# Expert blocks of 1792 columns in place of 896 in the MoE stage of a two-layer decoder trunk

## The reference

```
def swiglu(x, w_gate, w_up, w_down):
    return (jax.nn.silu(x @ w_gate) * (x @ w_up)) @ w_down

def moe_swiglu(x, w_router, w_gate, w_up, w_down):
    top_vals, top_idx = lax.top_k(logits, TOP_K)
    ...
    for e in range(N_EXPERTS):
        out = out + gates[..., e:e + 1] * swiglu(x, w_gate[e], w_up[e], w_down[e])
```

## Time and profile before

| | us |
|---|---|
| median of 3 runs | 1392.83 |
| lowest and highest run | 1390.17, 1393.66 |
| the profiled execution's own time | 1392.43 |
| its span in the trace | 1390.7 |
| first product of the expert stage to the last down matmul | 451.79 to 1352.9 |
| PE, DVE, ACT busy, share of the span | 96%, 83%, 71% |

### The profile page before, as it was taken

One profiled execution on the slowest core, in us unless ns is written; L12 is line 12 of the kernel. 1 busy time (PEld: TensorE's weight loads), 2 busy tenths in 40 slices (PEclk: granted clock), 3 DMA queues, 4 the chain that ended last, 5 costly groups with the idle time before them and its releaser, 6 DMA issues.

```text
span 1390.7 us, 19504 instructions
## 1 busy us (share of the span) xinstructions
PE 1332.4 (96%) x6863; PEld 1145.8 (82%) x6863; DVE 1147.9 (83%) x1052; ACT 990.2 (71%) x959; POOL 96.9 (7%) x112
## 2 busy tenths in 40 slices
PE   9999999999999999999999999999999998999987
PEld 8988888888997887878779888788888887787865
DVE  5776554466665898999999999999999999899986
ACT  5555444446555777888978888888888898787884
POOL 2000000000000086300000000000000002000000
PEclk9999999999999999999999999999999999999999
DMA  9657855567542799999999999999999999999980
GB/s 321 238 164 277 287 195 182 182 218 229 181 137 72 284 355 415 409 411 412 391 409 396 411 411 412 400 412 410 410 412 409 402 412 409 411 409 397 397 351 30
DMA packets 137062, 454.51 MB, mean 327 GB/s; under 512 B 8233, under 2 KB 29749, under 8 KB 124718
## 3 DMA queue, kind: packets, MB, share of 16 engines
q1 hardware_dynamic: 130272, 429.95, 80.6%
q0 software_dynamic: 4832, 17.13, 3.4%
q10 hardware_dynamic: 1902, 6.70, 1.4%
HBM read 437.99 MB, written 15.75 MB: 326 GB/s over the span
## 4 chain that ended last, share of the span: by engine, by line
PE 56%; DMA 18%; DVE 13%; issue 7%; ACT 5%; SPq 1%; ACTq 0%; DVEq 0%
PE banks L1228 15%; PE banks L1777 13%; DVE w_lo L2000 10%; DMA raw<-in_o_exp_down 8%; DMA raw<-in_o_exp_gate 7%; PE banks L1262 6%; PE banks L1798 5%; PE banks L1536 4%; PE banks L1850 4%; PE banks L1814 3%; ACT w_hi L684 3%; DMA raw<-in_e_w_in 1%; DMA raw<-in_o_exp_up 1%; PE banks L1761 1%; SPq L394 1%
## 5 line engine op out<-in xcount | busy, mean ns | idle before, releaser
L2000 DVE TENSOR_TENSOR w_lo<-raw,w_hi 128x1792 fp32r<-128x1792 f32 (+1 forms) x454 | 919.6, 2063 | 123.4 <-PE banks L1228 50.0
L684 ACT ACTIVATE w_hi<-raw 128x1792 fp32r<-128x1792 f32 (+1 forms) x454 | 784.1, 1736 | 273.3 <-PE banks L1228 79.7
L1798 PE MATMUL banks<-w_lo,x_hi 128*128 128x448 f32 x512 | 131.5, 379 | 18.7 <-DVE w_lo L2000 18.4
L1798 PEld LDWEIGHTS banks<-w_lo,x_hi 128*128 128x128 f32 x512 | 91.0, 188 | 45.4 <-DVE w_lo L2000 39.5
L1777 PE MATMUL banks<-w_hi,x_hi 128*128 128x448 f32 x512 | 127.5, 371 | 0.0
L1777 PE MATMUL banks<-w_lo,x_hi 128*128 128x448 f32 x512 | 125.1, 366 | 1.8 <-DVE w_lo L2000 1.8
L1798 PE MATMUL banks<-w_hi,x_hi 128*128 128x448 f32 x512 | 125.4, 367 | 0.0
L1777 PE MATMUL banks<-w_hi,x_lo 128*128 128x448 f32 x512 | 124.7, 365 | 0.0
L1228 PE MATMUL banks<-w_hi,x_lo 128*128 128x512 f32 (+1 forms) x304 | 108.5, 357 | 0.3 <-DVE x_lo L2035 0.3
L1228 PE MATMUL banks<-w_hi,x_hi 128*128 128x512 f32 (+1 forms) x304 | 108.1, 356 | 0.0
L1228 PE MATMUL banks<-w_lo,x_hi 128*128 128x512 f32 (+1 forms) x304 | 108.1, 356 | 0.0
(11 more groups left out here) (340 smaller groups left out, 1827.3 us busy)
## 6 DMA issues: line engine op xcount, KB each, us to landing
raw<-in_o_exp_gate SPq DMA_DIRECT2D x128, 896.0 KB, 8.1
raw<-in_o_exp_up SPq DMA_DIRECT2D x128, 896.0 KB, 8.8
raw<-in_o_exp_down SPq DMA_DIRECT2D x96, 1024.0 KB, 8.4
raw<-in_o_exp_down SPq DMA_DIRECT2D x32, 512.0 KB, 7.9
raw<-in_o_w_qkv SPq DMA_DIRECT2D x12, 1024.0 KB, 5.2
raw<-in_e_ffn_gate SPq DMA_DIRECT2D x11, 1024.0 KB, 5.1
raw<-in_e_ffn_up SPq DMA_DIRECT2D x11, 1024.0 KB, 5.3
raw<-in_e_ffn_down SPq DMA_DIRECT2D x11, 1024.0 KB, 5.0
```

The source lines that it names most:

```text
L684: act.activation(w_hi[:, at % HI, 0:size], raw[:, at % RAW, 0:size], ACT.Copy).then_inc(hi_made, 1)
L1798: mm = pe.matmul(bank[first + f][:, 0:CUT // 2], x_two[:, 2 * k + kk, :], w[:, kk, f * (CUT // 2):(f + 1) * (CUT // 2)], start=start and k ...
L2000: ve.tensor_tensor(w_lo[:, at % LO, 0:size], raw[:, at % RAW, 0:size], w_hi[:, at % HI, 0:size], ALU.subtract)\
```

## The change

`CUT` is 1792 and `BLOCKS` 2, so a superstep has 48 tiles and each duo two of them. A gate or up tile is now one 128-row chunk by 1792 columns: the same 896 KB, in rows of 7168 bytes. Tiles, bytes and matmuls of the stage stay as many as they were. A product fills four PSUM banks, gate and up one after the other in the same four; the other four hold the down sums. The loop over blocks is gone: the duo loop holds both supersteps. On ACT and DVE the merged element-wise operations cover twice the columns, in halves where a chain needs them so. The wide sums are cleared by two DVE memsets, where two zero matmuls did it.

The tiles of a superstep stand thus: 0 to 7 wide gate; 8, 9 small down (of the block before); 10 to 17 wide up; 18 to 21 small down; 22 to 29 small gate; 30, 31 small down; 32, 33 wide down; 34 to 41 small up; 42 to 47 wide down. Tiles 19, 31, 33 and 43 are single chunks (512 KB). `turn_wide` stands between 19 and 20, the first `turn_sums` after 31, the second after 43. At a duo's boundary all of `turn_rows` comes before tile 46 in one piece, and so do the ACT and DVE splits of the gathered rows.

```diff
-STEP_TILES = 24
-SKIP = 4
+STEP_TILES = 48
+SKIP = 8
...
-                load(tile_at(i, j, b), w[e, of, :, 2 * k:2 * k + 2], slot=(MOE_T - SKIP + i) % RAW)
+                load(tile_at(i, j, c), w[e, of, :, k:k + 1], slot=(MOE_T - SKIP + i) % RAW)
...
-                for k in range(4):
-                    up(eg, wide, of, k, k, j, b)
-                up(eu, wide, of, 0, 4, j, b)
-                down(small_was, of_was, 0, 5, j, b)
-                up(eu, wide, of, 1, 6, j, b)
-                down(small_was, of_was, 1, 7, j, b)
-                up(eu, wide, of, 2, 8, j, b)
-                up(eu, wide, of, 3, 9, j, b)
...
+                for k in range(KC):
+                    up(eg, wide, of, k, k, j, c)
+                small_down(0, 2)
+                for k in range(KC):
+                    up(eu, wide, of, k, 10 + k, j, c)
+                small_down(2, 6)
+                for k in range(KC):
+                    up(eg, small, of, k, 22 + k, j, c)
+                small_down(6, 8)
+                second_half(wide, small, of, j, c)
...
             with sp.Fori(0, last) as j:
                 wide, small = wide_of(j), small_of(j)
-                blocks(wide, small, j)
+                superstep(wide, 1, small, 0, small, j, 0)
                 sp.wait_ge(jobs_ready, 1)
                 wide, next_small = wide_of(j + 1), small_of(j + 1)
-                superstep(wide, 0, small, BLOCKS - 1, next_small, j, BLOCKS)
+                superstep(wide, 0, small, 1, next_small, j, 1)
...
+            def up_products(base, k, i, j, c, passes, free=None):
...
+                wait_high(tile_at(i, j, c))
+                for n, (x, low) in enumerate(passes):
+                    if low:
+                        wait_tile(tile_at(i, j, c))
+                    for f in range(4):
...
+                        mm = pe.matmul(bank[base + f][:, 0:CUT // 4], x, w[low][:, FOURTHS[f]],
+                                       start=k == 0 and n == 0, stop=k == KC - 1 and n == len(passes) - 1, skip_group_check=True)
+                mm.then_inc(tile_used, 1)
```

More of the change, by code:

```diff
@@ L487, in small_of @@
                 return sp.value_load(job_int[0:1, bass.ds(j + MOST, 1)], min_val=0, max_val=EXPERTS - 1)
[L489 to L497, removed]
+            for k in range(KC):
+                up(eg, 0, 0, k, 8 + k, None, None)
+            for k in range(KC):
+                up(eu, 0, 0, k, 16 + k, None, None)
             sp.wait_ge(ids_ready, 1)
             first_small = sp.value_load(job_int[0:1, MOST:MOST + 1], min_val=0, max_val=EXPERTS - 1)
-            for k in range(4):
-                up(eg, first_small, 0, k, 12 + k, None, None)
+            for k in range(KC):
+                up(eg, first_small, 0, k, 24 + k, None, None)
             second_half(0, first_small, 0, None, None)
@@ new lines, in st, with sts, silu_wide @@
+            def st(i, j, c, final=False):
+                used(i, j, c)
+                split_at(i + HI, j, c, final)
+            def sts(first, last, j, c, final=False):
+                for i in range(first, last):
+                    st(i, j, c, final)
+            def silu_wide(j, c):
+                if j is not None:
+                    act.wait_ge(hidT_ready, step_no(j, c) - 1)
+                for m in range(2):
+                    act.activation(halves(hid)[m], columns(0, m), ACT.Silu).then_inc(e_silu_made, 1)
@@ new lines, in turned_wide, with copy_sums, high_gate @@
+            def turned_wide(j, c):
+                act.wait_ge(hidT_ready, step_no(j, c))
+                for m, (first, last) in enumerate(CHUNKS):
+                    act.activation(hidT_hi[:, first:last], turned(1 if j is None else 0, m), ACT.Copy).then_inc(hidT_hi_made, 1)
+            def copy_sums():
+                for m in range(2):
+                    act.activation(halves_of_sums[m], columns(0, m), ACT.Copy).then_inc(s_copied, 1)
+            def high_gate(j, c):
+                act.wait_ge(fold_ready, 2 * step_no(j, c) - 1)
@@ L1166, in block @@
+                if c:
                     for half in range(2):
@@ L1816, in product @@
                     return mm
[L1818 to L1826 removed]
+                wait_high(tile_at(i, j, c))
+                if t == 7:
+                    wait_tile(tile_at(i, j, c))
@@ new lines, in los, with hidden_wide @@
+            def los(first, last, j=None, c=None, final=False):
+                for i in range(first, last):
+                    lo(i, j, c, final)
+            def hidden_wide(j, c):
+                n = step_no(j, c)
+                ve.wait_ge(tile_used, tile_at(23 if j is None else 17, j, c) + 1)
+                for m in range(2):
+                    ve.wait_ge(e_silu_made, 2 * n - (1 - m))
+                    ve.tensor_tensor(halves(hid)[m], halves(hid)[m], columns(1 if j is None else 0, m), ALU.mult).then_inc(e_hid_made, 1)
@@ new lines, in clear_wide, with second_half @@
+            def clear_wide(j=None):
+                for half in range(2):
+                    if j is not None:
+                        ve.wait_ge(y_made, 2 * j + (half + 1))
+                    ve.memset(bank[6 + half], 0.0).then_inc(wide_cleared, 1)
+            def second_half(j, c, final=False):
+                add_gate(j, c)
+                lo(32, j, c, final)
+                lo(33, j, c, final)
+                if c:
+                    fold_y(j)
+                for n, i in enumerate((34, 36, 38, 40)):
+                    if final:
+                        add_rows(*divmod(n, 2))
+                    los(i, i + 2, j, c, final)
+                lo(42, j, c, final)
+                lo(43, j, c, final)
+                add_up(j, c)
+                hidden_small(j, c)
+                lo(44, j, c, final)
+                low_small(j, c)
+                lo(45, j, c, final)
+                if j is not None and not c and not final:
+                    gathered(0, j + 1)
+                    gathered(1, j + 1)
+                    gathered_small(j + 1)
+                lo(46, j, c, final)
+                lo(47, j, c, final)
```

762 lines of the change are left out of this document (327 added, 435 removed).

## The result

The changed kernel takes **1426.46 us** (median of 4 runs, 1424.38 to 1428.18), the kernel before 1391.91 in the same comparison: 1.024 times as long, 95% interval 1.0218 to 1.0262. I had said 1395, 1376 to 1409. The direction I leaned to was right, the size was not, and the time lies outside my range.

A forecast was written before the change was run, and what follows sets the result against it. Fetch bounds the kernel before; PE and DVE would hide its saving. 100.7 + 753.2 + 19 + 4.8 + 18 = 895.7, plus 5.2 and 1.5, gave 902.4 against 901; +2.5 taken: about 1395 us, range 1376 to 1409.

The forecast's parts named there:

- What bounds before: Steady block of the kernel before: the fetch bounds it, 53.6 us, with PE and DVE 1.5 to 2 us behind.
- Part 1, the fetch: Gate and up rows of 7168 bytes for 3584: 18.4 us less fetch (0 to 25.6) over 16 blocks.
- Part 2: Engines in a long phase: a superstep walks to 107.6 us, so PE and DVE hide the fetch's saving.
- tiles 32 to 47: 36.6: Superstep's end: wide downs 19.2, small up 13 to 15.5 half hidden by the downs, two turns 3; together 36.6 us.
- Part 3: the boundary: Once a duo: fold and memsets 2.2 us, turning 1.4, wait for gathered rows 2.75; together 6.35.
- lump of 1.5 us: Whole stage: added for one more case than now of the granted clock falling behind an idle PE.
- Part 4: opening and tail: Stage's two ends: opening and its second half 100.7 us, tail 18.
- Rival A: Fetch stays the bound, rings carry DVE's lead through small phases: 1374 us, 1367 to 1385; chance 0.27.
- Rival B: Stalls at tiles 22 and 0 with the clock falling behind them, 1.6 us a superstep more: 1408 us; chance 0.18.
- Rival C: Pieces are cut into packets as before, fetch keeps its time: 1393 to 1403 us; chance 0.07.
- The signs I named: In the trace: `silu_wide` starts 107 to 109 us apart, DMA share 0.96 to 0.99, mean packet 5.4 KB or more, among others.
- stalls at every superstep, +1.7: Upper bound of the unknown sizes: 1.7 us more a superstep, +12 in all.

The follow-up runs named there:

- light turning: Changed kernel with 3 splits of gathered rows on ACT and on DVE at the boundary, and 3 transposes for 16 in each superstep: 1410.81 us.
- all light parts: Changed kernel with boundary splits and turning cut, fold at the superstep's end, small gate w_lo on half columns: 1404.58 us; with half of gate and up columns fetched, 1375.43.

## Why the prediction was wrong, step by step

- **What bounds before: right.** The fetch. Halving it gave 37 us; relief of DVE gave nothing. The floor that I read from busy times, 1.5 to 2 us under the fetch in a block, so 6 to 8 a duo, was near the 8.6 measured. But I read the earlier trace rows as evidence: SP's waits on DVE are 227 us before, 237 changed, and 228 with half the fetch. They are the ring's pace, whoever bounds, and tell nothing.
- **Part 1, the fetch: right in kind, 14 for 18.4.** And nearly all of it is hidden in the changed kernel, as said (2.6 us left).
- **Part 2: two thirds of the walk held.** Tiles 0 to 17: 42.6 walked, 19.4 + 3.6 + 19.5 = 42.5 measured. Tiles 18 to 31: 28.3 walked, 28.5 to 29.0 measured, with the wait at tile 22 at 2.0 for 1.7 and DVE's pace through the small gate at 1.9 a tile; moving the low half showed that the wait is DVE's amount of work. **The step that failed is "tiles 32 to 47: 36.6".** With the fold's 2.2 and the turning's 1.4 of part 3, I had 76.8 for them in the two supersteps of a duo; without the boundary's wait they took 82.0 to 83.0, 17 us more over three duos. I summed the work there and named no wait. In the duo from 673.83 there are these: for `add_gate` and the tiles' w_lo 1.2, for `add_up` ahead of turning 1.6, and turning stands twice at 1.7 where I had it once at 1.4. (The runs with half the fetch and with light turning say that these two are not the engines' own cost: one goes when tiles land early, the other is waited for anyway.) The fold cost 2.3 there as walked, and 2.6 to 2.7 in the other two duos, where the clock fell behind it. A new product must wait for the one before to leave the four banks; the walk priced that at one of three places. What the sharing costs is read from the timeline alone.
- **Part 3: the boundary, 6.35 walked.** The wait of 2.75 was 2.7 to 2.9. I left the clock to a lump of 1.5 us for the whole stage. It cost 1.7 and 1.9 at two of the three boundaries, nothing at the third, and 3 at the scatter.
- **Part 4: opening and tail, 118.7 walked.** The opening took 108.5 for 100.7: the memsets and the low half stand on DVE ahead of the small tiles there, PE waited 3.6 and then 1.0 for its turn of sums, and the clock fell behind it (14 turns took 2.9 for 1.55). The tail took 23.1 for 18, with the scatter behind a wait of 3.25 and at the lower clock:

```profile
1371.50 6.63 PE L1731 MATMUL quad<-work 128*128 128x512 f32 x8 [3.25 <-ACT work L1103]
```

- **The sum.** Opening 108.5, six supersteps 687.8, the last 115.0, tail 23.1: 934.4, for 100.7 + 664.6 + 112.4 + 18 = 895.7. That is 38.7 missed, 23.2 of it in the six supersteps, 7.8 in the opening, 5.1 in the tail. I had added 6.7 in lumps and taken 1 more, so 31 us stayed out.
- **Rival A** fell: supersteps of 113.5 to 115.8, not 105. **Rival B** had both places right (tiles 22 and 0) and said that the clock would fall behind them. It did in three of seven and in two of three cases, and cost something at tile 0 only. B said 1408, with 1.6 a superstep beyond my walk; the six took 3.9 each beyond it. **Rival C** fell: 6362 bytes a packet.
- **The signs I named:** share 0.98 and mean packet as said; starts of `silu_wide` 113 to 117 apart, not 107 to 109. My range ended at +12, "stalls at every superstep, +1.7"; the order had three places to stall, and I bounded one.

## What to carry to other kernels

A reordering is judged by its engines' floor, and that is measured by taking the other bound away: halving the fetch in both orders told in one pair what eight runs on single waits did not. A trial of an order in a kernel that another bound holds shows nothing below its slack. When one buffer (here four banks) serves product after product, list every change of hands with its chain of copy, turn and subtract, and put a price at each; a walk that sums work between them is a lower bound. Single waits taken away don't add up: behind each stands the next bound. And before a few microseconds are credited to an edit, the granted clock of both traces is compared stretch by stretch.

## What the runs showed of the hardware that I had not expected

- A loop's return can cost an engine 3 to 5 us without a wait on anything. PE's did, once its loop over duos held two supersteps of code (4.94, 4.20, 3.23 and 2.95 in the traces; 15 us in all with what follows it). The profile does not show what the time goes to. ACT's return took 5.45 us in the changed kernel, where the w_hi tiles ahead hid it from PE. With all light parts it took 6.45, and the eight wide gate tiles there took 21.0 and 21.3 us for 19.5:

```profile
790.46 1.70 ACT L692 ACTIVATE w_hi<-raw 128x1792 fp32r<-128x1792 f32 x1 [6.45 <-issue]
```

- The clock's fall behind an idle PE is not a fixed price of the wait. Behind 2.73 us of idle PE the granted clock of the next 2 us read 0.50 at one boundary and 1.00 at another; behind 2.0 us in front of w_lo it stayed at 1.00 in one duo and fell to 0.50 in two; behind 1.8 us at tile 22 it fell in three supersteps of seven, and cost nothing there, because DVE set the pace.
- A DMA share near 1 is no proof that the fetch bounds: q1 was 97.1% busy with 166.37 MB in 430 us, 387 MB/ms, while at 99.9% it moved 144.47 MB in 352, 410. A packet of the same length was busy 255 ns in one and 247 in the other.
